# Sixteen of eighty modulation sums moved from VectorE to GpSimd and ScalarE

## The reference, cut to what matters

```python
cond_lat = silu(c)                                   # [1, 1024]
mod_l = (cond_lat @ w_mod[i] + b_mod[i])[:, None, :] # [1, 6 * 1024], for each of the two layers i
sh1, sc1, g1, sh2, sc2, g2 = jnp.split(mod_l, 6, axis=-1)
a_lat = _modulate(x, norm_mix_g[i], sh1, sc1)        # rmsnorm(x) * (1 + sc1) + sh1
y_lat, y_ctx = _mla(a_lat, a_ctx, pos, ...)          # layer 0: attention with 8 heads over 512 keys
x = x + g1 * y_lat
y = _hier_moe(f_lat, ...)                            # 32 experts, 2 for each token
x = x + g2 * y
```

## Time and profile before

| what | us |
|---|---|
| median of 3 runs | 2275.02 |
| lowest, highest | 2272.23, 2277.49 |
| profiled execution | 2279.97 |
| its span | 2278.2 |
| TensorE busy in it | 1990.2 (87%) |
| VectorE busy | 1211.2 (53%) |
| ScalarE busy | 804.4 (35%) |
| GpSimd busy | 28.2 (1%) |
| moved from HBM | 658.22 MB, 289 GB/s over the span |

### The profile page before, as it was taken

One profiled execution on the slowest core, in us unless ns is written; L12 is line 12 of the kernel. 1 busy time (PEld: TensorE's weight loads), 2 busy tenths in 40 slices (PEclk: granted clock), 3 DMA queues, 4 the chain that ended last, 5 costly groups with the idle time before them and its releaser, 6 DMA issues.

```text
span 2278.2 us, 45305 instructions
## 1 busy us (share of the span) xinstructions
PE 1990.2 (87%) x17682; PEld 1534.8 (67%) x17685; DVE 1211.2 (53%) x2486; ACT 804.4 (35%) x1557; POOL 28.2 (1%) x39
## 2 busy tenths in 40 slices
PE   7989887667879988666678999998999999998998
PEld 3567554434549855333446888887888888887887
DVE  3798221111237622111125767878668767878666
ACT  2233110000024411000004655556555655556554
POOL 0000000000000000000000000000001000100000
PEclk9999999888889999888898999999999999999999
DMA  9789999999996699999999646244556556244641
GB/s 404 301 340 392 429 431 431 431 432 431 431 431 271 259 420 432 431 432 431 432 431 344 221 140 212 93 158 139 174 157 206 185 156 215 93 143 135 202 144 61
DMA packets 240816, 660.83 MB, mean 290 GB/s; under 512 B 6448, under 2 KB 202048, under 8 KB 210752
## 3 DMA queue, kind: packets, MB, share of 16 engines
q1 hardware_dynamic: 240240, 657.25, 73.4%
q10 hardware_dynamic: 464, 2.05, 0.2%
HBM read 658.22 MB, written 1.06 MB: 289 GB/s over the span
## 4 chain that ended last, share of the span: by engine, by line
PE 61%; DMA 21%; DVE 11%; issue 2%; ACT 2%; SPq 2%; another core or an unknown queue 1%; DVEq 0%; ACTq 0%; PEldq 0%
PE ps L2395 19%; DMA A<-in_moe_w_up 12%; PE ps L2400 10%; PE ps L1748 7%; DMA ring<-in_moe_w_up 6%; PE ps L2721 4%; PE ps L1777 3%; DVE ring L546 3%; DMA arena<-in_moe_w_up 2%; SPq L3300 2%; PE ps L1730 1%; PE ps L1698 1%; PE ps L2180 1%; PE ps L2182 1%; PE ps L2181 1%
## 5 line engine op out<-in xcount | busy, mean ns | idle before, releaser
L2395 PE MATMUL ps<-XS,WS 128*128 128x512 f32 x1280 | 451.8, 398 | 8.2 <-DVE WS L2376 8.0
L2376 DVE TENSOR_TENSOR WS<-ring,WS 128x1024 fp32r<-128x1024 f32 (+1 forms) x272 | 324.1, 1193 | 178.0 <-ACT WS L2371 177.4
L2371 ACT CAST WS<-ring 128x1024 fp32r<-128x1024 f32 (+1 forms) x272 | 278.8, 1026 | 264.5 <-PE ps L2400 260.3
L2400 PE MATMUL ps<-XS,WS 128*128 128x256 f32 x1280 | 358.3, 280 | 0.0
L2028 DVE TENSOR_TENSOR RS<-RS,ps 64x256 f32<-64x256 f32 x70 | 29.6, 422 | 579.6 <-ACT RS L1837 579.6
L1748 PE MATMUL ps<-ring,RS 128*32 128x256 f32 x2176 | 239.1, 448 | 90.8 <-DMA ring<-in_moe_w_up 33.0
L2395 PEld LDWEIGHTS ps<-XS,WS 128*128 128x128 f32 x1280 | 240.4, 188 | 69.6 <-issue 5.9
L2400 PEld LDWEIGHTS ps<-XS,WS 128*128 128x128 f32 x1280 | 241.5, 189 | 0.0
L1748 PEld LDWEIGHTS ps<-ring,RS 128*32 128x32 f32 x2176 | 126.3, 128 | 155.1 <-issue 134.0
L2395 PE MATMUL ps<-HS,WS 128*128 128x512 f32 x616 | 217.1, 397 | 0.0
L1748 PE MATMUL ps<-arena,RS 128*32 128x256 f32 x1120 | 168.3, 467 | 48.5 <-DMA A<-in_moe_w_up 23.7
(11 more groups left out here) (411 smaller groups left out, 3527.5 us busy)
## 6 DMA issues: line engine op xcount, KB each, us to landing
ring<-in_ffn_w_gu SPq DMA_DIRECT2D x88, 1024.0 KB, 7.3
arena<-in_moe_w_down SPq DMA_DIRECT2D x32, 2048.0 KB, 48.7
ring<-in_moe_w_up SPq DMA_DIRECT2D x32, 2048.0 KB, 47.8
ring<-in_moe_w_down SPq DMA_DIRECT2D x32, 2048.0 KB, 47.7
ring<-in_moe_w_gate SPq DMA_DIRECT2D x32, 2048.0 KB, 46.5
ring<-in_ffn_w_down SPq DMA_DIRECT2D x32, 1408.0 KB, 6.4
ring<-in_mod_later SPq DMA_DIRECT2D x20, 2048.0 KB, 10.3
SPARE<-in_moe_w_gate SPq DMA_DIRECT2D x16, 2048.0 KB, 43.7
```

The costliest lines, as they stand in the source:

```text
L2371: L.inc(L.eng.copy(self.parts(u)[0], source), self.w_high)
L2376: L.inc(L.eng.tensor_tensor(wl, self.unit(u)[1], high(wh), ALU.subtract), self.w_split)
L2395: L.eng.matmul(ps[:, bank, :].rearrange("p (j t) -> p j t", j=2), wh[:, i, :], moving[:, :, k, :], start=k == 0, stop=False)
L2400: mm = L.eng.matmul(ps[:, bank, 0:TL], wl[:, i, :], moving[:, 0, k, :], start=False, stop=k == total - 1)
```

## The change

Later tiles 8, 10, 12 and 15 (`POOLED`, all of layer 1) are no longer stepped on VectorE. GpSimd multiplies their 16 blocks by the condition row (`multiply`, the first thing in its stream), a block at a time as the tiles land. ScalarE adds up the products with a copy that accumulates (`accumulate`), two blocks after each of the eight output copies. A slot of a pooled tile comes free with ScalarE's fourth sum. VectorE adds the bias of these columns later, in `second_layer`, with one small addition for each tile.

VectorE keeps 16 tiles (`KEPT`), 64 steps. Up to step 28 nothing moves. Then a pair has six steps (in place of ten), the last pair three (in place of five), and the output tiles 14 (in place of 16).

```diff
@@ -514,18 +514,26 @@
 
             SLOTS = [(0, s) for s in range(4, 12)] + [(1, s) for s in range(12)]
             TILES = 4
-            STEPS = TILES * len(SLOTS)
+            POOLED = (8, 10, 12, 15)
+            KEPT = (0, 1, 2, 3, 4, 5, 6, 7, 9, 11, 13, 14, 16, 17, 18, 19)
+            STEPS = TILES * len(KEPT)
             FIRST_LAYER = TILES * 8
 
             def __init__(self):
                 self.cond_row = sig("later_cond_row")
                 self.summed = sig("later_summed")
+                self.multiplied = sig("later_multiplied")
+                self.accumulated = sig("later_accumulated")
                 self.slots = []
 
             def plan(self, *places):
                 for at in places:
                     i = len(self.slots)
-                    self.slots.append(plan(piece("mod_later", i), (1, self.TILES * D), (self.summed, self.TILES * (i + 1)), at))
+                    if i in self.POOLED:
+                        freed = (self.accumulated, self.TILES * (self.POOLED.index(i) + 1))
+                    else:
+                        freed = (self.summed, self.TILES * (self.KEPT.index(i) + 1))
+                    self.slots.append(plan(piece("mod_later", i), (1, self.TILES * D), freed, at))
 
             def make_cond_row(self, L):
 
@@ -535,7 +543,7 @@
             def steps(self, L, first, last):
 
                 for n in range(first, last):
-                    i, t = n // self.TILES, n % self.TILES
+                    i, t = self.KEPT[n // self.TILES], n % self.TILES
                     l, s = self.SLOTS[i]
                     if n == 0:
                         L.eng.wait_ge(self.cond_row.sem, 1)
@@ -545,6 +553,41 @@
                     rows = slot(self.slots[i])[:, t * D:(t + 1) * D]
                     L.inc(L.eng.tensor_tensor_reduce(out=rows, in0=rows, in1=COND_ROW, scale=1.0, scalar=vcol("b_mod", 1, 48 * l + c),
                                                      op0=ALU.mult, op1=ALU.add, accum_out=MOD[l][:, c, 0:1]), self.summed)
+
+            def pooled_rows(self, n):
+
+                i, t = self.POOLED[n // self.TILES], n % self.TILES
+                return slot(self.slots[i])[:, t * D:(t + 1) * D]
+
+            def pooled_column(self, n):
+
+                return self.TILES * self.SLOTS[self.POOLED[n // self.TILES]][1] + n % self.TILES
+
+            def multiply(self, L):
+
+                L.eng.wait_ge(self.cond_row.sem, 1)
+                for n in range(self.TILES * len(self.POOLED)):
+                    if n % self.TILES == 0:
+                        slot_ready(L, self.slots[self.POOLED[n // self.TILES]])
+                    rows = self.pooled_rows(n)
+                    L.inc(L.eng.tensor_tensor(rows, rows, COND_ROW, ALU.mult), self.multiplied)
+
+            def accumulate(self, L, first, last):
+
+                for n in range(first, last):
+                    L.eng.wait_ge(self.multiplied.sem, n + 1)
+                    rows, c, l = self.pooled_rows(n), self.pooled_column(n), self.SLOTS[self.POOLED[n // self.TILES]][0]
+                    L.inc(L.eng.activation(rows, rows, ACT.Copy, accum_out=MOD[l][:, c, 0:1]), self.accumulated)
+
+            def add_pooled_bias(self, L, tiles):
+
+                L.eng.wait_ge(self.accumulated.sem, self.TILES * (self.POOLED.index(tiles[-1]) + 1))
+                for i in tiles:
+                    l, s = self.SLOTS[i]
+                    c = self.TILES * s
+                    o = MOD[l][:, c:c + self.TILES, 0]
+                    L.inc(L.eng.tensor_tensor(o, o, vcol("b_mod", self.TILES, 48 * l + c), ALU.add))
+                L.join()
 
         RAW_HIGH = place("RAW_HIGH", [P, KD, TL + 4], F32R, spare_at)
         RAW_LOW = place("RAW_LOW", [P, KD, TA], F32R, XT_at)
@@ -1126,6 +1169,7 @@
 
 
             PAIRS, UNITS_Q = 4, 8
+            ACCUMULATED = (0, 2, 4, 6, 8, 10, 12, 14, 16)
 
             def __init__(self, later):
                 self.later = later
@@ -1408,10 +1452,12 @@
                     if p + 1 < self.PAIRS:
                         copy_rope(p + 1)
                     copy_outputs(u)
+                    self.later.accumulate(L, *self.ACCUMULATED[u:u + 2])
                     copy_turned(u + 1)
                     if p + 1 < self.PAIRS:
                         exps(u + 2)
                     copy_outputs(u + 1)
+                    self.later.accumulate(L, *self.ACCUMULATED[u + 1:u + 3])
                 for m in range(KD):
                     L.eng.wait_ge(self.y_added.sem, m + 1)
                     if m == 0:
@@ -1500,16 +1546,15 @@
                     largest(u + 1)
                     later.steps(L, done, done + 1)
                     normalise(u + 1)
-                    later.steps(L, done + 1, done + 5)
-                    done += 5
+                    later.steps(L, done + 1, done + 3)
+                    done += 3
                     if p + 1 < self.PAIRS:
                         rotate(p + 1)
-                        later.steps(L, done, done + 2)
+                        later.steps(L, done, done + 1)
                         largest(u + 2)
-                        later.steps(L, done + 2, done + 3)
                         normalise(u + 2)
-                        later.steps(L, done + 3, done + 5)
-                        done += 5
+                        later.steps(L, done + 1, done + 3)
+                        done += 3
 
                 L.eng.wait_ge(self.outs_copied.sem, self.UNITS_Q)
                 L.eng.wait_ge(later.summed.sem, later.FIRST_LAYER)
@@ -1534,6 +1579,7 @@
             def second_layer(self, L):
 
                 L.eng.wait_ge(self.later.summed.sem, self.later.STEPS)
+                self.later.add_pooled_bias(L, self.later.POOLED)
                 for which in range(2):
                     L.inc(make_gain_lat(L, 1, which))
 
@@ -3322,6 +3368,7 @@
         @block.gpsimd
         def _(pool):
             L = Lane(pool, line["pool"], spare)
+            later.multiply(L)
             for m in moes:
                 m.pool(L)
             counted = [(s, s.n) for s in Signal.made]
```

## The result

The changed kernel takes 2301.57 us (median of 4 runs, 2297.18 to 2305.60) against 2276.26 us (4 runs, 2272.23 to 2281.12) of the kernel before on the same chip. The ratio is 1.0104, interval 1.009 to 1.0119: 24 us slower, between 20 and 27. The forecast was 2292.9 us, in a range of 2274 to 2304. The direction was right, and the time lies in the range, near its upper end. The size was short by about a quarter: of the two terms of the sum the release came out at 5.3 us against 5.4, attention at 20.0 against 12.5.

What follows compares the result with a forecast made beforehand. The start of the expert weights' transfer stream was taken to bound the kernel. Attention +12.5 and release +5.4 gave +17.9 us, 2292.9 us from the median of 2275.02; range 2274 to 2304, this case alone 2283 to 2304.

Steps and rivals of the forecast that it cites:

- What bounds the kernel: First expert stage: a transfer stream whose end moves one for one with its start, and what follows moves along.
- the argument from holes: Transfers in attention: holes of 11.7 us in 105 to 123 and 7.5 us after; the first expert stage has none.
- Steps taken off: VectorE in attention: 14 steps fewer, 16.8 us; TensorE gains at most 3.7 us of waits, 2.5 taken.
- Sums on ScalarE: After each output copy: two passes of 1.15 us, 18.4 us in all, fit idle time; taken as nothing.
- Products on GpSimd: Sixteen 128x1024 products in attention: 2.0 to 2.8 us each, 2.3 taken, 37 us in all.
- What the products do to VectorE: Attention: steps beside products cost 1.2 + 2.2 us; end of attention moves +8 to +19.5, +12.5 taken with thinning.
- The rule that I set aside: VectorE's two-port mode also locked: one scaling a tile waits 2.2 us more; the sum would be 4 us higher.
- What the release does: Tile 19 waits for the last sum: output weights at copy + 14.8, expert stream 5.4 us later; bounds 0 and 9.8.
- Bias additions: Four small additions in the routing, 0.2 us apiece, 0.8 us ahead of the experts, hidden by 9 us of cover.
- The first: Rival, no blocking of VectorE's steps in attention: -2.5 + 5.4 = +2.9, 2277.9 us; chance 0.18.
- The second: Rival, compute paces the first experts and is faster, needing no blocking too: 2269 to 2270 us; chance 0.13.
- The third: Rival, blocked GpSimd's products reach ScalarE late and stretch attention on top: 2297 to 2310 us; chance 0.08.

Runs made afterwards that it cites:

- p1: Kernel before, all VectorE steps kept, plus sixteen 128x1024 GpSimd products on parts of tiles nobody reads: 2308.91 us, ratio 1.013.
- b2: Kernel before, with the first expert tile loaded ahead of the second query weights: 2270.62 us, ratio 0.9972.
- b1: Kernel before, with later tile 10 loaded ahead of the second query weights: 2275.79 us, ratio 0.999.
- x1: Changed kernel without products: GpSimd clears one column of each block in place of multiplying 1024: 2284.26 us, ratio 1.0024.
- x6: Changed kernel, complete, each GpSimd product of 1024 columns issued as four of 256: 2290.09 us, ratio 1.0053.
- x3: Changed kernel, with the second half of the output weights ahead of later tile 19 in SyncE's list: 2297.43 us, ratio 1.0081.
- x4: Changed kernel without products and with the second half of the output weights ahead of later tile 19: 2278.84 us, ratio 1.0006.
- x5: Changed kernel, GpSimd multiplying each block by the constant 0.5 in place of the condition row: 2286.29 us, ratio 1.0036.
- a1: Changed kernel unaltered, run once more: 2303.96 us, ratio 1.0105.
- x2: Changed kernel, each GpSimd product covering 256 of the 1024 columns: 2285.60 us, ratio 1.003.
- b3: Kernel before, later tile 10 and first expert tile ahead of second query weights, output weights' second half ahead of tile 19: 2271.48 us, ratio 0.9979.

## Why the prediction was right in direction and short in size

*What bounds the kernel.* The end of the first expert stage moves one for one with the start of its stream: in p1 both attention and the stage end 29.1 us later, and in the changed kernel the weights land 25.3 us later and the stage ends 25.3 us later. What follows moves along less exactly: after, 25.3 at the stage and 24.2 at the end; p1, 29.1 and 24.5; b2, -5.0 and -7.5. p1 still has 28.6 at GpSimd's first subtractions of the second stack, 26.1 and 23.8 at the next two groups, in the stretch that drifts in the changed kernel too; these are single executions. Over all runs p1 is 30 us above before (25 to 34) and b2 6.4 below (3.9 to 9.1), which fits the stage's shifts. What I had too simple is the argument from holes: b1 shows that a hole ahead of the last release is worth nothing by itself.

*Steps taken off.* I took 2.5 us of TensorE's 3.7 us of waits. x1 shows 2.5, of which 2.0 are waits (8.8 to 6.8).

*Sums on ScalarE.* Taken at nothing. They cost 1.05 us each from start to start, under the 1.15 assumed, and in x1, which has all 16, attention is 2.5 us shorter. Two of them in the changed kernel:

```profile
131.12 1.06 ACT L580 ACTIVATE ring<-ring 128x1024 f32<-128x1024 f32 x1
132.08 0.19 ACT L580 ACTIVATION_READ_ACCUMULATOR ring<-ring 128x1 f32 x1
132.17 1.04 ACT L580 ACTIVATE ring<-ring 128x1024 f32<-128x1024 f32 x1
```

*Products on GpSimd.* 2.3 us forecast from quarter-size rows, 2.34 measured as the shortest, 2.53 as the median beside VectorE. The first tile landed later than forecast (108.4, not 106), its loading having taken 8.8 us and not the shortest 7.6.

*What the products do to VectorE.* This is the step that failed in its size: +15.0 us for four tiles, less 2.5, was the term, and 20.0 came. The mechanism is right. The stretch rows split the 20.0: TensorE's waits grew by 13.5 us, where the sum had 12.5, and its clock cost 6.5, where the sum had nothing. So what was missing is not the blocking but what a long wait does to the engine behind it: the term put TensorE's time at its waits alone. x6 shows the same from the other side: the products' bytes unchanged, each wait short, the clock at 1.00 and 6.3 us saved by that alone. x3 shows it by accident: equal waits in sum, in shorter pieces, 4.3 us less busy. And x4 shows a lower clock behind a wait of 3.86 us with no product in the kernel. The profile of before could not have given the number, its clock being 1.00 in all four windows, but it could have warned: a forecast in which one tile holds VectorE up for 8.8 us, where TensorE's longest wait in attention was 1.7, has to carry a charge for the clock.

That the waits came so near is partly luck, for their make-up was other than I wrote. Adding up over the timeline what VectorE's instructions took beyond their usual length gives 24.2 us: 10.5 in five steps, 1.9 in the rotations, but 8.3 in three groups of scalings and 3.5 in four negations of 128x2. Half lies in operations that the sum had not charged. The forecast had 4 x 5.5 = 22 us of it in the steps and rotations, and 15.0 of that reaching TensorE; against x1 TensorE's waits grew by 22.3 - 6.8 = 15.5. The rule that I set aside for want of a row, that VectorE's two-port mode is locked out as well (the Trainium skill, SBUF — State Buffer, section SBUF: two separate sides), is what these rows show: a scaling, 0.485 us as a median, took up to 2.58. By that rule the sum would have been 4 us higher, 2297 from the median in place of 2293; the waits alone would then have been overstated, 16.5 against 13.5. Against one part of that page a run speaks: that a GpSimd instruction holds the pair for its whole length. In x5 one of 2.77 us delayed VectorE by at most 0.8.

*What the release does.* Forecast: the weights at copy + 14.8 and 5.4 us for the stage. Measured 14.7 and 5.3 (a1: 5.2; x5: 5.1; x6: 5.4). With attention short it is more, 7.5 in x1 and 7.3 in x2, a dependence that the sum had not got: it took the shortest loading, 7.6 us, for tile 19, which in x1 took 9.9, tile 18 being still under way when it was issued. x3 takes 3.0 us of it away and p1 all of it.

*Bias additions.* Hidden as forecast. The stage's shift beyond attention is the weights' later landing and nothing else: 14.7 - 9.4 = 5.3 us after, and in x1, where the weights come 16.9 us after the copy, 16.9 - 9.4 = 7.5.

*Rivals.* The first, no blocking, had the sum of x1: it gave +2.9 and x1 measured 5.5 (1.0024, 3.2 to 7.5), 2.6 us more, of which 2.1 are the release (7.5 against 5.4). Its condition, no blocking, was not met: the steps are stretched. The second needed no blocking and a stage paced by compute; neither was so, and in x1, with blocking gone, the shortened VectorE still gave no gain over before. The third did not come about: ScalarE's sums found their products ready, though GpSimd's tiles took up to 11.8 us for four.

## What to carry to other kernels

A product of two SBUF operands moved to GpSimd did not run beside VectorE but in front of it. Charge every VectorE instruction of the kinds stretched here (two SBUF operands, or a scaling from SBUF to SBUF) with the rest of the GpSimd instruction under way, and if it must be so, cut the GpSimd work into short instructions (here 1.0104 became 1.0053 with 256 columns in place of 1024). When a forecast lengthens TensorE's waits, look at their single length as well as at their sum, and read busy and idle of equal work from one window before and after, beside its granted clock: with that below 1.00, the difference in busy was the clock's price here. And where a queue is taken in order, moving bytes into a hole helps only if they leave the part of the queue behind the last late release; b2 did that with one tile and is, with b3, the fastest kernel here.

## What the runs showed of the hardware that I had not expected

- A GpSimd operation of one operand over 128x1024 (2.77 us) is longer than the product with two (2.34 us), and yet lets VectorE in: waits of 0.8 us at most against 2.2.
- A VectorE negation of 128x2 values waits as well (0.17 us became 1.05, and 1.32 at 181.50), while a reciprocal of 128x2 with a product under way keeps its 0.15: it is the kind that is held up, not the amount.
- TensorE's granted clock fell after it had waited 3.34, 6.92 and 5.84 us in attention, and groups of matmuls then took 3.50, 3.78 and 3.63 us in place of 1.95, 1.98 and 2.02. In x6, with waits of up to 3.2 us there, it did not fall; in x4, without products, it fell after one of 3.86.
- The custom multiply-and-sum has VectorE busy 1.28 us but leaves 1.20 from start to start; blocked, it takes up to 3.46.
